# Gate and up projections of two FFN chunks as seven block products of 256 tokens instead of eight

## What is computed

```python
def swiglu(x, w_gate, w_up, w_down):          # w_gate, w_up: 1024 x 2816, w_down: 2816 x 1024
    return (jax.nn.silu(x @ w_gate) * (x @ w_up)) @ w_down
...
x = layer_norm(ALPHA * x + 0.5 * swiglu(x, ffn1_w_gate[l], ffn1_w_up[l], ffn1_w_down[l]), ln1_g[l], ln1_b[l])
```

## Time and profile before

| | |
|---|---|
| median of 3 runs | 1225.65 us (1225.61 to 1225.9) |
| profiled execution, its own time | 1225.59 us |
| its span, first to last instruction | 1223.9 us (1.7 us lie around it) |
| PE busy | 1210.0 us, 99% of the span, 5915 matmuls |
| DVE busy | 784.7 us, 64% |
| ACT busy | 514.4 us, 42% |
| POOL busy | 111.4 us, 9% |
| chain that ended last | 96% PE |
| mean granted TensorE clock | 0.999 |

### The profile page before, as it was taken

The page is one execution under the profiler, slowest core; times in us unless marked ns, Lnnn a source line. Parts: engine busy times, 40 slices in busy tenths (PEclk is TensorE's granted clock), DMA queues, the critical chain, the costliest instruction groups (busy, mean ns, idle before and its releaser), DMA issues.

```text
span 1223.9 us, 16099 instructions
## 1 busy us (share of the span) xinstructions
PE 1210.0 (99%) x5915; PEld 1020.9 (83%) x5915; DVE 784.7 (64%) x1132; ACT 514.4 (42%) x821; POOL 111.4 (9%) x128
## 2 busy tenths in 40 slices
PE   8999999999999999999999999999999999999997
PEld 8888888888889888888888888888988888888886
DVE  5374747565867767777764586555747474747486
ACT  5142424242436767667643225341323242424243
POOL 1101010101013000111010020001210101010101
PEclk9999999999999999999999999999999999999999
DMA  9938392928167313212273516214564838383811
GB/s 292 307 88 224 71 237 69 240 69 239 35 190 230 99 52 104 70 52 69 70 223 103 172 37 187 78 44 120 190 172 106 204 88 220 86 223 73 235 18 69
DMA packets 175812, 166.97 MB, mean 136 GB/s; under 512 B 5888, under 2 KB 147216, under 8 KB 174736
## 3 DMA queue, kind: packets, MB, share of 16 engines
q1 hardware_dynamic: 162064, 126.92, 34.5%
q0 software_dynamic: 13488, 39.33, 14.7%
q10 hardware_dynamic: 208, 0.01, 0.0%
HBM read 137.93 MB, written 7.34 MB: 119 GB/s over the span
## 4 chain that ended last, share of the span: by engine, by line
PE 96%; ACT 1%; DVE 1%; DMA 1%; SPq 0%; issue 0%; DVEq 0%; ACTq 0%
PE bank L885 19%; PE bank L887 18%; PE bank L886 18%; PE banks_scores L887 8%; PE banks_scores L886 8%; PE banks_scores L885 8%; PE bank L892 6%; PE banks_scores L892 3%; PE bank L1261 1%; PE banks_scores L1232 1%; PE bank L911 1%; DMA xa<-in_x 1%; PE bank L1281 1%; PE banks_scores L1233 1%; PE bank L1280 1%; PE banks_scores L911 0%
## 5 line engine op out<-in xcount | busy, mean ns | idle before, releaser
L885 PE MATMUL bank<-xT_hi,ring_hi 128*128 128x512 f32 (+1 forms) x680 | 261.1, 384 | 0.3 <-DVE gate L2552 0.3
L887 PE MATMUL bank<-xT_hi,ring_lo 128*128 128x512 f32 (+1 forms) x680 | 259.0, 381 | 0.0
L886 PE MATMUL bank<-xT_lo,ring_hi 128*128 128x512 f32 (+1 forms) x680 | 258.8, 381 | 0.0
L1971 DVE TENSOR_TENSOR ring_lo<-raw,ring_hi 128x1024 fp32r<-128x1024 f32 x171 | 207.8, 1222 | 48.6 <-ACT ring_hi L1525 48.2
L1525 ACT ACTIVATE ring_hi<-raw 128x1024 fp32r<-128x1024 f32 x171 | 179.4, 1057 | 136.6 <-PE bank L887 79.1
L887 PEld LDWEIGHTS bank<-xT_hi,ring_lo 128*128 128x128 f32 x680 | 127.8, 188 | 24.7
L885 PEld LDWEIGHTS bank<-xT_hi,ring_hi 128*128 128x128 f32 x680 | 128.0, 188 | 24.0 <-issue 0.7
L886 PEld LDWEIGHTS bank<-xT_lo,ring_hi 128*128 128x128 f32 x680 | 128.0, 188 | 23.3
L885 PE MATMUL banks_scores<-xT_hi,ring_hi 128*128 128x512 f32 (+1 forms) x384 | 142.8, 372 | 0.0
L887 PE MATMUL banks_scores<-xT_hi,ring_lo 128*128 128x512 f32 (+1 forms) x384 | 142.6, 371 | 0.0
L886 PE MATMUL banks_scores<-xT_lo,ring_hi 128*128 128x512 f32 (+1 forms) x384 | 142.6, 371 | 0.0
(11 more groups left out here) (382 smaller groups left out, 2268.8 us busy)
## 6 DMA issues: line engine op xcount, KB each, us to landing
raw<-in_ffn_w_gate SPq DMA_DIRECT2D x44, 512.0 KB, 7.1
raw<-in_ffn_w_up SPq DMA_DIRECT2D x44, 512.0 KB, 6.4
wd<-in_ffn_w_down SPq DMA_DIRECT2D x20, 1024.0 KB, 5.0
raw<-in_mix_w_in SPq DMA_DIRECT2D x34, 512.0 KB, 3.9
t<-in_ffn_w_down SPq DMA_DIRECT2D x20, 512.0 KB, 6.4
t<-wd POOLq DMA_DIRECT2D x11, 512.0 KB, 5.2
wd<-wd POOLq DMA_DIRECT2D x10, 512.0 KB, 8.1
t<-t POOLq DMA_DIRECT2D x10, 512.0 KB, 9.6
```

Source lines behind the costliest of these rows:

```text
L885: pe.matmul(dst, hi, mhi, start=start, stop=False)
L886: pe.matmul(dst, hi, mlo, start=False, stop=False)
L887: return pe.matmul(dst, lo, mhi, start=False, stop=stop)
L1971: nc.vector.tensor_tensor(dst, src, hi.bitcast(F32), ALU.subtract).then_inc(done, 1)
```

## The change

Two chunks (256 gate columns and 256 up columns) become a **group**: the matrix [gate | up] of 1024 x 512 is cut into blocks 11, 12 (rows 0 to 511: gate, up) and 21, 22 (rows 512 to 1023), x transposed is cut likewise into halves of rows and of tokens, and seven block products are made (q = 0 to 6, in the order 0, 1, 4, 3, 5, 2, 6), each with 256 tokens moving. Chunks 0 and 1 stay plain (`P`); groups 1 to 10 are the other twenty. The list of an FFN is written out by `ffn_sequence` and unrolled on all engines in place of the loop; it has 4 plain units, 70 group units, 35 down units (`D`, as before) and 2 last units (`L`).

- Weight sums: POOL adds 11+12 and (11+12)+22 with two of its own instructions (128x1024 each) and issues two accumulating DMAs (into 12 and into 21). The group's four blocks fill the four raw buffers; block 11 of the next group waits for the split of unit q=3, block 12 for q=5, block 22 for q=2, block 21 for q=6. The down sums stay DMAs, in another order.
- Sums of x blocks: ten DVE additions of 128x1024 and four high/low splits at the start of each FFN (`x_first_sum` ... `x_fourth_sum`, `x_high`, `x_low`).
- Corners: ACT copies the accumulating bank after q = 0, 4 and 5 (`snapshot`), DVE adds or subtracts the product in the other bank (`corner_first`, `corner_last`, `corner_second`), ACT applies Silu (in place of Sigmoid, so that one DVE multiplication a chunk goes), DVE multiplies (`group_hidden`).
- The scaling of the residual goes from DVE to ACT (`scale_block`). Products 2 and 6 of the last quad stay in their PSUM banks and last tiles are accumulated on them; tiles in the order 0, 1, 2, 3, 5, 7, 4, 6.

```diff
+ORDER = (0, 1, 4, 3, 5, 2, 6)
+def ffn_sequence():
+    order = [("P", 0, j) for j in range(PLAIN)]
+    order += G(1, 0, 1, 4, 3, 5) + D(0, 0) + G(1, 2, 6)
+    for d in range(1, QUADS):
+        a, b, done = 2 * d, 2 * d + 1, d - 1
+        order += G(a, 0, 1) + (D(done, 0) if d > 1 else [])
+        order += G(a, 4, 3) + D(done, 1) + G(a, 5) + D(done, 4) + G(a, 2, 6) + D(done, 3)
+        order += G(b, 0, 1, 4, 3) + D(done, 5) + G(b, 5) + D(done, 2) + G(b, 2, 6) + D(done, 6)
+    a, done = GROUPS, QUADS - 1
+    order += G(a, 0, 1) + D(done, 0) + G(a, 4, 3) + D(done, 1) + G(a, 5) + D(done, 4) + G(a, 2) + D(done, 3) + G(a, 6)
+    order += D(done, 2, 5, 6)
+    return order + [("L", 0, r) for r in range(2)]
+BLOCKS = {"11": 3, "12": 5, "22": 2, "21": 6}
```

On POOL:

```diff
+            def gate_sums(f, g):
+                landed_block(f, g, "11")
+                landed_block(f, g, "12")
+                if g > 1:
+                    pool.wait_ge(unit_lo, ffn_unit(f, "G", g - 1, 3) + 1)
+                nc.gpsimd.tensor_tensor(gate_t1[:, :], b11, b12, ALU.add).then_inc(gate_sum[0], 1)
+                landed_block(f, g, "22")
...
+                nc.gpsimd.tensor_tensor(gate_t2[:, :], gate_t1[:, :], b22, ALU.add).then_inc(gate_sum[1], 1)
+                pool.dma_start(b12, b22, accum_op=ALU.add).then_inc(gate_sum[2], 16)
...
+            def gate_sum_21(f, g):
...
+                pool.wait_ge(unit_lo, ffn_unit(f, "G", g, 1) + 1)
+                pool.dma_start(raw_at((f, g, "21")), gate_t2[:, :], accum_op=ALU.add).then_inc(gate_sum[3], 16)
```

On PE:

```diff
+                def corners_free(g, q):
+                    k = 3 * group_no(f, g)
+                    if q == 0:
+                        pe.wait_ge(*((silu_done, hidden_count(f, g - 2) + 2) if g > 2 else (h_full, hidden_count(f, 0) + 1)))
+                    elif q == 1:
+                        pe.wait_ge(*((corner, k - 2) if g > 1 else (h_full, hidden_count(f, 0) + 2)))
...
+                    elif q == 2:
+                        pe.wait_ge(corner, k + 2)
+                        pe.wait_ge(x_sum_lo, 4 * f + X_LOWS[f][q])
...
+                def group_product(g, q):
+                    x_hi, x_lo = x_part(f, q)
+                    for e in range(2):
+                        dst = bank({1: 3, 2: 2, 3: 2}.get(q, g % 2))[:, WINDOW * e:WINDOW * (e + 1)]
+                        cols = slice(P * e, P * (e + 1))
+                        for k in range(4):
+                            for a, b in ((hi, x_hi), (hi, x_lo), (lo, x_hi)):
...
+                                mm = pe.matmul(dst, a[:, k, cols], b[:, k, :], start=fresh, stop=True, skip_group_check=True)
...
```

On ACT, at the start of an FFN:

```diff
...
+                prep(n0 + 4)
+                x_high(3)
+                prep(n0 + 5)
+                x_high(4)
+                silu(0)
+                if f == 0:
+                    for n in range(T_MEM, T_X1):
+                        turned_high(n, mem0_hi, (n - T_MEM) // 2)
+                prep(n0 + 6)
+                scale_block(0)
+                prep(n0 + 7)
+                scale_block(1)
+                if f == 0:
+                    x_high(2)
+                silu(1)
+                prep(n0 + 8)
...
```

On DVE, at the start of an FFN:

```diff
...
+                split(n0 + 4)
+                x_first_sum()
+                split(n0 + 5)
+                x_second_sum()
+                hidden(0)
                 if f == 0:
                     for n in range(T_MEM, T_X1):
-                        turned_low(n, memT_hi, memT_lo, (n - T_MEM) // 2)
+                        turned_low(n, mem0_hi, mem0_lo, (n - T_MEM) // 2)
+                split(n0 + 6)
+                x_low(4)
                 split(n0 + 7)
+                x_low(3)
+                if f == 0:
+                    x_fourth_sum()
+                hidden(1)
                 split(n0 + 8)
+                x_third_sum()
...
```

More of the change, by code:

```diff
@@ L157, in raw_tables @@
     where, count, before, last, used = {}, {}, {}, {}, {}
-    for n, at in order:
-        where[n], before[n] = at, last.get(at)
+    for key, at, reader in order:
+        where[key], before[key] = at, last.get(at)
         used[at] = used.get(at, 0) + 1
-        count[n], last[at] = 16 * used[at], n
+        count[key], last[at] = 16 * used[at], reader
     return where, count, before
@@ L586, in _, with load @@
         def _(sp):
-            def load(n, src, form=None, i=None):
+            def load(n, src, form=None):
                 dst = raw_at(n)
@@ L643, in ffn_units @@
[L643 to L653 removed]
+                for name in BLOCKS:
+                    block(1, name)
@@ new lines, in end_tile @@
+                def end_tile(j):
+                    n, b, half = ffn_unit(f, "L", 0, 0), j // 2, j % 2
+                    if j < 4:
+                        pe.wait_ge(end_lo_done, 2 * f + 1)
+                    else:
+                        pe.wait_ge(end_lo_done, 2 * f + 2)
+                    if j == 0:
+                        pe.wait_ge(corner, 3 * group_no(f, GROUPS) + 3)
+                    elif j in (5, 7):
+                        pe.wait_ge(end_sums, 8 * f + {5: 2, 7: 4}[j])
+                    fresh = j in (0, 2, 5, 7)
+                    tok = slice(b * P, (b + 1) * P)
+                    for m in range(2):
+                        ready(n + m)
+                        hi, lo = (r[:, half * HALF:(half + 1) * HALF] for r in parts(n + m))
+                        form = end_hi[:, m, tok], end_lo[:, m, tok], hi, lo
+                        if fresh:
+                            mm = split_product(end_bank(j), *form, m == 0, m == 1)
+                        else:
+                            mm = added_product(end_bank(j), *form)
+                    mm.then_inc(*((unit_used, 2) if j == TILE_ORDER[-1] else (end_tiles, 1)))
@@ L960, in half_units @@
+                def half_units(n, side, part, units=range(2)):
                     toks = token_half(part)
@@ L1036, in first_units_2 @@
                         half_units(n0 + 2 * side, side, 1)
-                def down_product(n, j, m, dst, first=True):
-                    b, half = j // 2, j % 2
-                    hi, lo = (r[:, half * HALF:(half + 1) * HALF] for r in parts(n + m))
-                    tok = slice(b * P, (b + 1) * P)
-                    form = end_hi[:, m, tok], end_lo[:, m, tok], hi, lo
-                    return split_product(dst, *form, m == 0, m == 1) if first else added_product(dst, *form)
-                last = sums_base(f) + 14 * (QUADS - 1)
@@ new lines, in end_low, with end_tile @@
+                def end_low(p):
+                    toks = token_half(p)
+                    dve.wait_ge(end_hi_done, 2 * f + 1 + p)
+                    low(end_lo[:, :, toks], hf[:, 0:2, toks], end_hi[:, :, toks], end_lo_done)
+                def end_tile(j):
+                    cols = slice(HALF * (j % 2), HALF * (j % 2 + 1))
+                    if j == TILE_ORDER[-1]:
+                        dve.wait_ge(unit_used, ffn_unit(f, "L", 0, 1) + 1)
+                    else:
+                        dve.wait_ge(end_tiles, 7 * f + TILE_ORDER.index(j) + 1)
+                    dve.wait_ge(sums, last + (8 if j < 4 else 10))
+                    nc.vector.scalar_tensor_tensor(out=x[:, j // 2, cols], in0=x[:, j // 2, cols], scalar=1.0,
+                                                   in1=end_bank(j), op0=ALU.mult, op1=ALU.add,
+                                                   accum_out=row_sum[:, j:j + 1]).then_inc(end_sums, 1)
@@ L2640, in _ @@
             turned_pair(T_X3, 3)
-            scale_residual(xb, range(TB), T_X3, (sums, 4))
             ffn(1, U_FFN2, xb)
```

1117 lines of the change are left out of this document (582 added, 535 removed).

## The result

The changed kernel took **1238.83 us** (median of 4 runs, 1237.71 to 1240.66) beside 1225.63 us for the kernel before on the same chip (1225.57 to 1225.9): ratio 1.0109, 95% interval 1.0091 to 1.0126. It is slower by 13.2 us. I had forecast 1220.0 with a range of 1210 to 1231; slower had a chance of 0.19. The forecast is wrong, and so is its range.

The account below looks back on a forecast made before the run. PE, busy 99% of the span, was taken to bound the kernel; -32.4 (PE) + 15.2 (first start) + 0.5 (clock) + 8.1 (second start) + 3.2 (ends) = -5.4 us, from 1225.6 to 1220.2 us, range 1210 to 1231.

Parts of the forecast that it names:

- PE's gain: Group products in both FFNs: 24 matmuls of 0.120 us, 2.88 us a product, together -32.4 us if PE never waits.
- The port term: Quads: POOL's four additions hold DVE for their full 2.39 us each, giving DVE 54.7 of 59.4 us.
- I find 1.2 used at worst: Quads, ahead of corner_last for product q=2: DVE's lateness uses at most 1.2 of 1.36 us of room.
- Cost in the steady state: nothing: Quads: PE never waits, with the ring as cover for late blocks; 0 us.
- The fourth rival: Every group: corner_last too late, one whole addition in the way, 1.03 us x 20 groups, 1241 us; chance 0.15.
- The second start: Start of FFN 2: PE waits 2.2 and 2.6 for hidden(0) and hidden(1), 3.3 for the first op_lo; +8.1 us.
- The first start: Start of FFN 1: PE waits 4.7 and 8.8 for hidden(0) and hidden(1), 1.7 for x_low(5); +15.2 us.
- The clock: First start: PE starts low behind the 8.8 us wait, mostly hidden in the next wait; between 0 and 3, taken +0.5 us.
- The ends: Ends of both FFNs: PE waits 1.3 us for end_low(0), twice, and 0.6 at the last tile; +3.2 us.
- DVE is not held up: Rival: POOL's additions do not hold DVE; first start 3.6 us shorter, second 0.6, 1216.0 us; chance 0.16.
- The starts hide: Rival: waits for hidden and x parts in the starts come early, whole gain shows, 1193 to 1203 us; chance 0.06.
- Block 21 late: Rival: in the first start block 21's load takes 15.5 instead of 6.3 us, start 6 to 7 us later, 1226.5; chance 0.13.

Follow-up runs that it names:

- e1: Changed kernel with POOL's two weight sums cut to one column of 1024 from group 2 on (output not the layer's): 1224.17 us.
- e2: Changed kernel with POOL's second addition for odd groups held until the last corner of the even group before, accumulating transfer issued ahead of it: 1232.42 us.
- e3: Changed kernel with throwaway matmuls on a free bank filling PE's waits in both starts: 1236.68 us.
- e8: Changed kernel with down product D(4,5) moved ahead of the first four end tiles on PE: 1236.64 us.
- e6: Changed kernel with ACT's and DVE's start lists reordered, and POOL's second addition of odd groups from group 3 on behind the last corner before: 1219.73 us.
- e7: Changed kernel with chunks 2 and 3 plain again, fourth x sum before third, POOL's second addition of odd groups behind the last corner: 1211.03 us.
- e9: e7 with D(4,5) ahead of the first four end tiles and POOL's group 2 additions ahead of the down blocks' second accumulating transfer: 1207.96 us.

## Why the prediction was wrong

**PE's gain** was right: 0.120 us a matmul, 2.88 us a product, -32.4 us. One small thing was not in it: a matmul of 512 behind one of 256 starts 0.03 us late, once in a down unit, 1.8 us in the quads of both FFNs.

**The port term** had the right sign, and it is the heart of the matter. "I take 2.39 ... DVE then has 54.7 of 59.4 us" was too high as a sum (51.6 to 52.0 measured; by e1 the four additions of a quad cost DVE 5.5 us and not 9.6), since not every addition meets an operation with two inputs in SBUF.

The step that failed is the next one, "**I find 1.2 used at worst**" of the 1.36 us of room ahead of `corner_last`, and with it "Cost in the steady state: nothing": it cost 1.02 us in 8 groups. Two of the signs that I had named for being wrong came with it, quads above 60 us and the wait for `corner`. I had reasoned that POOL adds "while other units run". In the even groups that have a group behind them neither addition does. The first falls some 8 us ahead of the corner and holds DVE for 2.22 us, which uses up all the room (e2). The second is released by the split of the product q=6 of the group before, which stands five DVE operations ahead of the corner, meets the split between them and holds it for 1.01 us, and that is PE's wait. In odd groups the second addition waits longer for its block and starts behind the corner (at 126.06, the corner at 125.24), so that 8 groups are hit and not 20.

The fourth rival named the place and the mechanism. Its size, "with one whole addition of 2.39 in the way it is 1.03 us", meets the 1.02 by luck: in the way are parts of two additions, 3.2 us together. Its 1241 lies near the 1238.8 by luck as well, with 20.6 us at the corner where 8.2 were measured. I gave it 0.15. The release times of the additions stood in the code; working them out would have moved 8.2 us from the rival into the sum.

**The second start** was short by 6.4 us. The waits for `hidden(0)` and `hidden(1)` came as computed (2.25 and 2.38, predicted 2.2 and 2.6). The wait for the first `op_lo` was to be 3.3 and was 5.24 with a slow down product behind it. The step "Behind it DVE has 6 operations of 1.14, five sums and two of 0.60 ... 14.8 us" left out POOL's additions for group 2, 4.2 us of holds; e1 took 4.4 us off this start. (By the prediction's own prices that sum is 14.3 and not 14.8.) The other 2.5 is the clock, shown by e3.

**The first start** was right to 1.4 us, though in other pieces: 2.75 for `hidden(0)` (predicted 4.7), then 1.49 of slow matmuls and 7.02 (8.8), then 1.38 of slow matmuls and 2.28 (1.7), and 1.57 of slow matmuls behind that (0.5). `x_low(5)` came at 64.8 where I had 64.4. I had not counted the hold of 2.2 us on it, and it was made up by DVE's being quicker before.

**The clock**, "between 0 and 3, I take +0.5": it was 1.6 us behind the last wait of the first start and 2.5 in the second, where I had nothing. The argument that most of it hides in the next wait was right, but a start has a last wait, and behind that nothing hides it.

**The ends** came as predicted: 1.57 each beyond the pitch in place of 1.3, and 0.9 for 0.6 in the tail. **The memory keys** were missed: PE waits 0.98 us at 377.18 for a split that stands on DVE behind the normalisation of the first blocks and is done at 377.13. With the kernel before no such wait stands in this place. That the order of the end tiles put DVE behind is argued from the timeline and was not tried.

**The sum against the range.** Of the 20.7 us between the two columns of the table 8.2 are the corner, 6.4 the second start, 1.4 the first, 1.8 the down units, 1.7 the memory keys and 1.2 the ends. All have one sign. The corner and 4.2 us of the second start come from working with DVE's operations at their undisturbed length, but for the additions of group 1; most of the rest is the clock and small terms that were put at nothing.

**The other rivals.** "DVE is not held up" is out. "The starts hide" is out. "Block 21 late" is out: its split stood 2.08 us, for ACT, which made it right behind `x_high(3)` without waiting for a landing.

## What to carry to other kernels

When work is given to GpSimd beside a VectorE that is nearly full, its time is charged to VectorE wherever it meets an operation there with two SBUF inputs (here 5.5 us of 9.6 in a quad), and *when* it is released decides whether that costs anything: set its release behind the operation with the least slack, not where its buffers come free, and look again after each move, also for additions that were always there (e8). A change that removes PE's cover at the start of a loop should be priced by the other engines' lists up to the first product of the new form; here one more plain pair of chunks in each FFN cost 3.2 us of PE's gain and still made the kernel 8.7 us faster (e6 to e7). And where PE waited 2.3 us or more, the matmuls behind the last wait ran slow as well (1.6 and 2.5 us here).

## What the runs showed of the hardware

- The hold works both ways between DVE and POOL, as the first start of the changed kernel shows (DVE's timeline, then POOL's):

```profile
25.22 3.40 DVE L2179 TENSOR_TENSOR x_sum<-xT_lo 128x1024 f32<-128x1024 f32 x1
...
61.24 3.41 DVE L2089 TENSOR_TENSOR xT_lo<-x_diff,xT_hi 128x1024 fp32r<-128x1024 f32 x1
```

```profile
24.80 2.73 POOL L799 TENSOR_TENSOR gate_t<-gate_t,raw 128x1024 f32<-128x1024 f32 x1 [2.40 <-DMA raw<-in_ffn_w_up]
...
60.31 3.25 POOL L794 TENSOR_TENSOR gate_t<-raw 128x1024 f32<-128x1024 f32 x1 [0.80 <-issue]
```

  DVE's operations of 1.22 us take 3.4, POOL's of 2.38 take 2.7 to 3.3. With two additions back to back the one DVE operation between them took 4.67 (e7). Two additions to `xa` with one input in PSUM, at 94.51, kept their pace of 0.60 us during an addition.
- PE's clock fell to 1.2 GHz behind waits of 2.3 us and more, and it stayed at 2.4 GHz behind the waits of 0.86 us in the quads and of 1.41 us at the ends. In between the same wait goes either way: after 2.25 us, at 903.28, the product still took 2.95 us and the next one, behind another 2.38 us, 4.41; in e8 the product behind the same wait, there 2.27 us, took 4.4 at once.
- The runs of the changed kernel scatter by 3 us (1237.71 to 1240.66), those of the kernel before by 0.3, those of e9 by 0.4. The excess of the first start alone was 17.1 us in one execution and 15.1 in another (e8, which has the same start). I take it that where the additions meet DVE depends on landings; no run shows that.
